# Sixteen experts in fp32 on one Trainium2 core: units of 64 tokens on two strips instead of units of 32 on four

## The chip, the cores and the metric

One core of one Trainium2 chip runs the kernel. The metric is device time in microseconds (us): the kernel before takes 1808.73 us, the median of 3 runs that lie between 1807.75 and 1811.84.

## The reference, cut to what matters

Two decoder layers over 576 tokens (512 of a prompt, 64 of a sample) of width 1024. Each layer is a mixer (convolution and forgetting attention in layer 0, sparse attention in layer 1), and behind it a mixture of experts, which the change concerns. All is float32.

```python
# hier_moe: m = 576 tokens, d = 1024, 16 experts with a hidden width of 512
g_w, g_idx = lax.top_k(softmax(x2 @ w_group + b_group), 1)        # one group of four
top_v, top_i = lax.top_k(e_logits[inside that group], 2)          # two experts inside it
combine = one_hot(expert_id) weighted by softmax(top_v) * g_w
for e in range(16):
    hid = silu(x2 @ w_gate[e]) * (x2 @ w_up[e])
    y = y + combine[:, e:e+1] * (hid @ w_down[e])
```

Each token is in two experts, so there are 1152 pairs of a token and an expert in a layer, spread unevenly.

## The kernel before, in words

The expert stage stands once in each layer. The sixteen experts are taken in 16 steps. Step s has room for `32 * UNITS[s]` tokens, with `UNITS = (3, 3, 5, 2, 4, 2, 4, 2, 3, 3, 2, 3, 3, 2, 3, 3)`, 47 units of 32 in all, and the experts are laid on steps by their size. Tokens beyond that room would go through `spilled`, which has turns of its own.

For each step GpSimd gathers the token rows from DRAM (`xg`, one indirect DMA; a second one for the step of five units), TensorE transposes them in eight 128-column pieces (`turn_x`, L1045), VectorE multiplies them by the norm's gain on the way out of the banks (`inputs`, L1981, into `xgt`). The weights of a step are three blocks of 2 MB (gate, up, down); they are streamed by SyncE into two sets of slots, and the load of a block for step s waits until the last unit of step s-2 has used the same slot (L506). SP issues them in order, so a wait for one block holds all that follow.

TensorE then takes one unit g (32 tokens) after another (`experts`, L1076). A unit is:

- gate: 8 chunks of the width x 4 strips. The stationary operand is 32 tokens x 128 rows, and the moving operand 128 columns of the weights. Strip j of the array (32 of its columns) makes features 128j to 128j+127, so four matmuls with an output of 32 partitions each stand side by side (`group_features`, L1068, the matmul on L1072).
- `turn_hid(g-1)`: one 128x128 transposition of the hidden tile of the unit before (L1084). In the last unit of a step, `turn_x` for the next step stands right behind it (L1115), and so ahead of up.
- up: as gate, into another bank.
- `down(g-1)`: 4 chunks x 4 strips with 256 moving columns (L1096), for the unit before.

In fp32 the profile records each of these matmuls twice, with a weight load (LDWEIGHTS) before each. So a unit has 64 + 64 + 32 = 160 recorded matmuls and as many weight loads.

ScalarE makes silu of gate (L1515), copies down's result to one of four buffers `y2` (L1506) and issues its store to DRAM, `expert_rows`. VectorE copies the transposed hidden tile (`turned`, L1989), multiplies silu by up (L2003), and does the inputs of the next step before that product (L1999). At the stage's start it also builds the token lists of steps 2 to 15: `list_places` for five token tiles behind units 0, 1 and 2; TensorE sums them in `lists` behind `down` (L1123 to L1130) and `list_order` (L1909) gives GpSimd the row numbers for the gather of step 2 and of all later ones. Only steps 0 and 1 start without these lists. After the last unit, `combine` gathers each token's two rows and adds them.

All engines wait on semaphore counts that are written out by hand, by unit number.

Of the kernel before, what the change touches and what calls it, by code (L numbers as in the profile page):

```python
# [26 lines left out]
NT = 5  # L27
# [9 lines left out]
NE = 16  # L37
# [20 lines left out]
GROUPS = sum(UNITS)  # L58
NROWS = 32 * GROUPS
STEP_OF = tuple(s for s in range(NE) for _ in range(UNITS[s]))  # L60
# [34 lines left out]
for _n, _w in (("H", NT * D), ("XT", DC * TOK), ("RING", RING * 4096), ("CR", 8192), ("A3", NT * 512),  # L95
# [9 lines left out]
    (sum(UNITS), "gate_mm up_mm down_mm silu hid ht_mm ht_ev y_ev"),  # L105
# [16 lines left out]
              "y_rows": tuple(16 * len(range(i, sum(UNITS), 4)) for i in range(4))}  # L122
# [13 lines left out]
def trunk(nc, a, o):  # L136
# [161 lines left out]
    y2 = [at("X", 5632 + 256 * i, 256) for i in range(4)]  # L298
    sil2, hid2, ht2 = [[at("X", c + 128 * i, 128) for i in range(2)] for c in (6656, 6912, 7168)]
# [107 lines left out]
    def _(sp):  # L407
# [86 lines left out]
        def experts(l):  # L494
# [33 lines left out]
        for b, name in ((3, "gate_mm0"), (1, "up_mm0"), (2, "down_mm0")):  # L528
            k = first_block(1, "in") + b
            sp.wait_ge(S(name), upto(name, FIRST[14] + UNITS[14]))  # L530
# [54 lines left out]
    def _(pool):  # L585
# [110 lines left out]
        def combine(l):  # L696

            pool.wait_ge(S(f"row_u{l}"), upto(f"row_u{l}", 1))
            for i in range(4):
                pool.wait_ge(S(f"y_rows{l}_{i}"), upto(f"y_rows{l}_{i}", 16 * len(range(i, GROUPS, 4))))  # L700
# [37 lines left out]
    def _(pe):  # L738
# [329 lines left out]
        def group_features(b, w, x):  # L1068

            for c in range(DC):  # L1070
                for j in range(4):
                    last = mm(bank(b, 0, 128, 32 * j, 32 * j + 32), x[:, c, :], w[:, c, 128 * j:128 * j + 128],  # L1072
                              start=(c == 0), stop=(c == DC - 1))
            return last

        def experts(l):  # L1076
# [5 lines left out]
            def turn_hid(g):  # L1082
                pe.wait_ge(S(f"hid{l}"), upto(f"hid{l}", g + 1))
                pe.transpose(bank(1 + g % 2, 128, 256), hid2[g % 2], ident).then_inc(S(f"ht_mm{l}"), 1)  # L1084

            def down(g):
                s = STEP_OF[g]
                if g == FIRST[s]:
# [13 lines left out]
            for g in range(GROUPS):  # L1102
                s = STEP_OF[g]
                u = g - FIRST[s]
                x = xgt[s % 2][:, :, 32 * u:32 * u + 32]
                if u == 0:
# [4 lines left out]
                group_features(0, g3(slot[s % 2][0], DC), x).then_inc(S(f"gate_mm{l}"), 1)  # L1111
# [4 lines left out]
                if u == 0:  # L1116
# [3 lines left out]
                group_features(1 + g % 2, g3(slot[s % 2][1], DC), x).then_inc(S(f"up_mm{l}"), 1)  # L1120
# [217 lines left out]
    def _(act):  # L1338
# [160 lines left out]
        def experts(l):  # L1499

            def store(g):
                i = g % 4
# [3 lines left out]
                af(y2[i], bank(3, 0, 256), ACT.Copy).then_inc(S(f"y_ev{l}"), 1)  # L1506
                act.wait_ge(S(f"y_ev{l}"), upto(f"y_ev{l}", g + 1))
                act.dma_start(y_d[32 * g:32 * g + 32, :].rearrange("t (q c) -> q t c", q=4), y2[i])\
                    .then_inc(S(f"y_rows{l}_{i}"), 16)

            for g in range(GROUPS):
# [3 lines left out]
                af(sil2[g % 2], bank(0, 0, 128), ACT.Silu).then_inc(S(f"silu{l}"), 1)  # L1515
# [4 lines left out]
        def spilled(l):  # L1520
            act.wait_ge(S(f"turns{l}"), upto(f"turns{l}", 1))
            for i in range(4):
# [923 lines left out]
```

## Time and profile before

| what | value |
|---|---|
| median of 3 runs | 1808.73 us |
| the profiled execution's own time | 1802.01 us |
| its span in the profile | 1800.2 us |
| TensorE busy (matmul) | 1475.0 us, 82% |
| TensorE instructions | 20035 matmuls, 20036 weight loads |
| VectorE, ScalarE, GpSimd busy | 652.6, 309.8, 146.8 us |
| TensorE matmuls on L1072 (gate and up) | 12032, 412.9 us |
| TensorE matmuls on L1096 (down) | 3008, 196.8 us |
| mean granted clock | 0.921 of 2.4 GHz |

A matmul's duration is its latency: those of different strips overlap, so busy times of lines are not shares of a whole. "issue" as a releaser of idle time means that no semaphore, engine or DMA in the profile released the instruction. The expert stages lie at about 528 to 884 us (layer 0) and 1405 to 1755 us (layer 1) of the span.

### The profile page before, as it was taken

The numbers are of one execution on the slowest core, as the hardware profiler recorded it, in microseconds if no ns is written. First come the engines' busy times: TensorE is split into PE (matmuls) and PEld (weight loads), VectorE is DVE, ScalarE is ACT, GpSimd is POOL, SyncE is SP. The second block draws the span as 40 slices with busy tenths as digits, with TensorE's granted clock in tenths as the row PEclk, the third lists the DMA queues.
The fourth block names the chain that finished last, engine by engine and source line by source line (L and its number), as shares of the span: only waits on it lengthen the run. The fifth ranks groups of instructions, "written<-read, shape, count | busy, mean of one in ns | idle before, by whom it ended". The sixth has DMA issues, their size and how long they took to land.

```text
span 1800.2 us, 46758 instructions
## 1 busy us (share of the span) xinstructions
PE 1475.0 (82%) x20035; PEld 958.8 (53%) x20036; DVE 652.6 (36%) x1574; ACT 309.8 (17%) x816; POOL 146.8 (8%) x370
## 2 busy tenths in 40 slices
PE   4999968889968988888459998888997798878880
PEld 2444534454467766767344333545545676766670
DVE  2029944331244211111155898665203431111114
ACT  2110024320100000000111211455301000000011
POOL 0039200000000000000110000000000100000002
PEclk9999878889859999999879998898996899999995
DMA  9131128774247788898520031333413568899945
GB/s 358 39 108 48 53 82 227 223 234 197 71 166 287 266 323 325 319 366 334 209 75 23 24 108 60 95 95 95 188 47 146 185 235 323 302 360 343 331 172 173
DMA packets 89531, 342.75 MB, mean 190 GB/s; under 512 B 22751, under 2 KB 39743, under 8 KB 75358
## 3 DMA queue, kind: packets, MB, share of 16 engines
q1 hardware_dynamic: 66254, 289.80, 44.8%
q0 software_dynamic: 10656, 37.56, 6.1%
q10 hardware_dynamic: 12408, 12.32, 2.0%
q8 instruction: 162, 2.65, 0.6%
q14 instruction: 51, 0.42, 0.1%
HBM read 309.53 MB, written 30.47 MB: 189 GB/s over the span
## 4 chain that ended last, share of the span: by engine, by line
PE 61%; DVE 16%; issue 9%; SPq 6%; DMA 4%; ACT 3%; POOL 1%; POOLq 0%; DVEq 0%; ACTq 0%
PE banks L1072 21%; PE banks L1096 9%; PE banks L1011 8%; DVE arena L2077 6%; PE banks L784 5%; PE banks L813 4%; SPq L438 3%; DVE arena L1626 3%; SPq L464 2%; PE banks L766 2%; PE banks L930 1%; PE banks L1051 1%; DMA arena<-expert_rows,arena 1%; PE banks L1084 1%; SPq L469 1%
## 5 line engine op out<-in xcount | busy, mean ns | idle before, releaser
L1072 PE MATMUL banks<-arena 128*32 128x128 f32 x12032 | 412.9, 278 | 76.4 <-issue 74.1
L1072 PEld LDWEIGHTS banks<-arena 128*32 128x32 f32 x12032 | 353.4, 111 | 115.8 <-issue 94.8
L1096 PE MATMUL banks<-arena 128*32 128x256 f32 x3008 | 196.8, 384 | 24.3 <-issue 23.5
L784 PE MATMUL banks<-arena 128*128 128x512 f32 (+1 forms) x400 | 174.0, 594 | 0.0
L1992 DVE COPY arena<-banks 128x128 f32<-128x128 f32 x94 | 27.4, 291 | 374.0 <-PE banks L1084 362.5
L1626 DVE TENSOR_TENSOR arena<-arena,banks 128x128 f32<-128x128 f32 (+4 forms) x118 | 44.1, 374 | 324.2 <-PE banks L1072 177.4
L1096 PEld LDWEIGHTS banks<-arena 128*32 128x32 f32 x3008 | 119.1, 111 | 65.8 <-issue 30.2
L813 PE MATMUL banks<-arena 128*128 128x512 f32 (+1 forms) x320 | 145.9, 602 | 0.0
L1011 PE MATMUL banks<-arena 128*128 128x512 f32 (+1 forms) x320 | 138.8, 594 | 1.4 <-issue 0.8
L1626 DVE TENSOR_TENSOR arena<-arena 128x256 f32<-128x256 f32 (+17 forms) x248 | 99.0, 432 | 87.7 <-ACT arena L1379 66.1
L784 PEld LDWEIGHTS banks<-arena 128*128 128x128 f32 (+1 forms) x400 | 70.7, 179 | 100.3 <-issue 100.2
L1626 DVE TENSOR_TENSOR arena<-banks,arena 128x512 f32<-128x512 f32 (+5 forms) x159 | 70.4, 473 | 138.9 <-ACT arena L1431 85.8
L1506 ACT ACTIVATE arena<-banks 128x256 f32<-128x256 f32 x94 | 36.0, 383 | 433.3 <-PE banks L1096 433.3
L2077 DVE SCALAR_TENSOR_TENSOR arena<-arena 128x512 f32<-128x512 f32 x120 | 105.2, 937 | 1.1
L1011 PEld LDWEIGHTS banks<-arena 128*128 128x128 f32 (+1 forms) x320 | 56.7, 179 | 82.1 <-issue 81.4
L813 PEld LDWEIGHTS banks<-arena 128*128 128x128 f32 (+1 forms) x320 | 55.6, 181 | 73.8 <-issue 72.2
L751 PE MATMUL banks<-arena 128*128 128x128 f32 (+1 forms) x160 | 29.6, 357 | 70.1 <-DVE arena L1656 70.1
L674 POOL DMA_INDIRECT arena<-hn_scratch,arena x32 | 29.5, 922 | 604.5 <-PE banks L1051 474.4
L1515 ACT ACTIVATE arena<-banks 128x128 f32<-128x128 f32 x94 | 26.1, 277 | 232.5 <-PE banks L1072 220.9
L751 PEld LDWEIGHTS banks<-arena 128*128 128x128 f32 (+1 forms) x160 | 25.9, 199 | 73.6 <-DVE arena L1656 51.5
L1414 ACT ACTIVATE arena<-arena 128x128 f32<-128x128 f32 (+3 forms) x96 | 53.0, 556 | 26.8 <-DVE arena L1675 26.8
L839 PE MATMUL banks<-arena 64*128 64x128 f32 (+3 forms) x192 | 41.1, 508 | 18.2 <-DVE arena L1675 16.8
(268 smaller groups left out, 1440.4 us busy)
## 6 DMA issues: line engine op xcount, KB each, us to landing
arena<-in_wstream SPq DMA_DIRECT2D x109, 2048.0 KB, 11.2
arena<-in_fox_kt SPq DMA_DIRECT2D x64, 256.0 KB, 3.0
arena<-in_fox_v SPq DMA_DIRECT2D x64, 256.0 KB, 3.0
arena<-in_dsa_page SPq DMA_DIRECT2D x64, 256.0 KB, 3.0
expert_rows<-arena ACTq DMA_DIRECT2D x94, 128.0 KB
expert_rows<-arena POOLq DMA_DIRECT2D x1, 6656.0 KB, 33.3
hn_scratch<-arena POOLq DMA_DIRECT2D x8, 512.0 KB, 3.7
arena<-in_x_prompt SPq DMA_DIRECT2D x1, 2048.0 KB, 10.0
```

Source lines behind the costliest of these rows:

```text
L438: return sp.value_load(pages[0:1, NPG * s + j:NPG * s + j + 1], min_val=0, max_val=a["n_pool"] - 1)
L464: sp.dma_start(g3(k_even[s % 2], NPG)[:, j, :], page_rows(a["fox_kt"], page_id(s, j)))\
L751: last = pe.transpose(bank(b, 128 * (c % 4), 128 * (c % 4) + rows(t)), hn[t % 2][0:rows(t), 128 * c:128 * c + 128], ident[0:rows(t), 0:row ...
L784: last = mm(bank(job % 4, 0, 512, 0, rows(t)), xt[:, c, c0:c1], w[:, c, :], start=(c == 0), stop=(c == DC - 1))
L813: last = mm(bank(job % 2, 0, 512, 0, rows(t)), xt[:, c, c0:c1], w[:, c, :], start=(c == 0), stop=(c == DC - 1))
L839: last = mm(bank(a, 0, n), q(2 * p + a)[:, 128 * t:128 * t + 128], k(2 * p + a)[:, 0:n], start=True, stop=(l == 1))
L1011: last = mm(bank(job % 4, 0, 512, 0, rows(t)), xt[:, c, c0:c1], w[:, c, :], start=(c == 0), stop=(c == DC - 1))
L1072: last = mm(bank(b, 0, 128, 32 * j, 32 * j + 32), x[:, c, :], w[:, c, 128 * j:128 * j + 128], start=(c == 0), stop=(c == DC - 1))
L1096: last = mm(bank(3, 0, 256, 32 * q, 32 * q + 32), ht2[g % 2][:, 32 * c:32 * c + 32], w[:, c, 256 * q:256 * q + 256], start=(c == 0), stop= ...
L1414: af(x, x, ACT.Exp, bias=mx[:, c:c + 1], scale=-1.0, accum_out=esum[:, c:c + 1])\
L1626: return v.tensor_tensor(out, x, y, op)
L2077: last = v.scalar_tensor_tensor(out=op, in0=ip, scalar=w, in1=op, op0=ALU.mult, op1=ALU.add)
```

## The change

A step's tokens are now taken in parts: as many of 64 tokens as fit, and a last one of 32 where `UNITS[s]` is odd. That makes 28 parts a layer (19 of 64 and 9 of 32) in place of 47 units. A part of 64 uses a stationary operand of 64 tokens on two strips of 64 columns each, with 256 moving columns in gate and up and 512 in down; a part of 32 is as before. `y2` becomes two buffers of twice the width. The transpositions of the next step's tokens move behind up (ahead of `down(g-1)`), and VectorE's inputs behind the product. The building of lists is packed into fewer, larger parts.

```diff
+PARTS = tuple((s, 64 * i, min(64, 32 * UNITS[s] - 64 * i)) for s in range(NE) for i in range((UNITS[s] + 1) // 2))
+GROUPS = len(PARTS)
+ENDS = tuple(sum((u + 1) // 2 for u in UNITS[:s + 1]) for s in range(NE))
...
-    y2 = [at("X", 5632 + 256 * i, 256) for i in range(4)]
+    y2 = [at("X", 5632 + 512 * i, 512) for i in range(2)]
...
-                    sp.wait_ge(S(name), upto(name, FIRST[s - 2] + UNITS[s - 2]))
+                    sp.wait_ge(S(name), upto(name, ENDS[s - 2]))
...
-        def group_features(b, w, x):
+        def part_features(b, w, x, n):
             for c in range(DC):
-                for j in range(4):
-                    last = mm(bank(b, 0, 128, 32 * j, 32 * j + 32), x[:, c, :], w[:, c, 128 * j:128 * j + 128],
+                for j in range(128 // n):
+                    last = mm(bank(b, 0, 4 * n, n * j, n * j + n), x[:, c, :], w[:, c, 4 * n * j:4 * n * j + 4 * n],
                               start=(c == 0), stop=(c == DC - 1))
...
             def turn_hid(g):
                 pe.wait_ge(S(f"hid{l}"), upto(f"hid{l}", g + 1))
-                pe.transpose(bank(1 + g % 2, 128, 256), hid2[g % 2], ident).then_inc(S(f"ht_mm{l}"), 1)
+                for i in range(PARTS[g][2] // 32):
+                    last = pe.transpose(bank(1 + g % 2, 256 + 128 * i, 384 + 128 * i),
+                                        hid2[g % 2][:, 128 * i:128 * i + 128], ident)
+                last.then_inc(S(f"ht_mm{l}"), 1)
...
                 for c in range(4):
-                    for q in range(4):
-                        last = mm(bank(3, 0, 256, 32 * q, 32 * q + 32), ht2[g % 2][:, 32 * c:32 * c + 32],
-                                  w[:, c, 256 * q:256 * q + 256], start=(c == 0), stop=(c == 3))
+                    j, i = divmod(c, n // 32)
+                    for q in range(128 // n):
+                        last = mm(bank(3, 0, 8 * n, n * q, n * q + n), ht2[g % 2][:, 128 * i + n * j:128 * i + n * j + n],
+                                  w[:, c, 8 * n * q:8 * n * q + 8 * n], start=(c == 0), stop=(c == 3))
...
-                if u == UNITS[s] - 1 and s + 1 < NE:
-                    turn_x(l, s + 1)
-                if u == 0:
+                if off == 0:
                     landed(s, 1)
                 if g > 1:
                     pe.wait_ge(S(f"ht_ev{l}"), upto(f"ht_ev{l}", g - 1))
-                group_features(1 + g % 2, g3(slot[s % 2][1], DC), x).then_inc(S(f"up_mm{l}"), 1)
+                part_features(1 + g % 2, g3(slot[s % 2][1], DC), x, n).then_inc(S(f"up_mm{l}"), 1)
+                if g == 2:
+                    for t in range(1, NT):
+                        lists(l, t)
+                if g == ENDS[s] - 1 and s + 1 < NE:
+                    turn_x(l, s + 1)
                 if g > 0:
                     down(g - 1)
                 if g == 1:
                     lists(l, 0)
-                if g == 2:
-                    lists(l, 1)
-                    lists(l, 2)
-                if g == 3:
-                    lists(l, 3)
-                    lists(l, 4)
...
+                i, r0 = g % 2, 32 * FIRST[s] + off
-                if g >= 4:
-                    act.wait_ge(S(f"y_rows{l}_{i}"), upto(f"y_rows{l}_{i}", 16 * (g // 4)))
+                if g >= 2:
+                    act.wait_ge(S(f"y_rows{l}_{i}"), upto(f"y_rows{l}_{i}", 16 * (g // 2)))
...
                 if g > 0:
                     turned(g - 1)
-                if g == FIRST[s] + UNITS[s] - 1 and s + 1 < NE:
-                    inputs(s + 1)
                 dve.wait_ge(S(f"up_mm{l}"), upto(f"up_mm{l}", g + 1))
                 dve.wait_ge(S(f"silu{l}"), upto(f"silu{l}", g + 1))
+                tt(hid2[g % 2][:, 0:4 * n], sil2[g % 2][:, 0:4 * n], bank(1 + g % 2, 0, 4 * n), ALU.mult)\
+                    .then_inc(S(f"hid{l}"), 1)
+                if g == ENDS[s] - 1 and s + 1 < NE:
+                    inputs(s + 1)
...
                 if g == 1:
-                    list_places(l, 1)
-                    list_places(l, 2)
+                    for t in range(1, NT):
+                        list_places(l, t)
                 if g == 2:
-                    list_places(l, 3)
-                    list_places(l, 4)
-                if g == 3:
                     list_order(l)
```

## Rows read from the trace of the kernel before

**Rows 1.** Stretches: length, busy of each engine (records), granted clock, DMA share, GB/s.

```profile
528.00:884.00 356.00, 304.90 (x7770) 250.49 (x7770) 63.35 (x177) 31.05 (x94) 13.72 (x15) 0.97 0.80 300
1405.00:1755.00 350.00, 298.06 (x7770) 245.72 (x7770) 63.38 (x177) 31.04 (x94) 13.71 (x15) 0.99 0.77 287
```

**Rows 2.** Groups by line, 528 to 884 us: count, busy, mean ns, idle before.

```profile
L1072 PE MATMUL banks<-arena 128*32 128x128 f32 x6016 | 208.9, 280 | 39.2 <-issue 38.0 <-DVE arena L1626 1.1
L1096 PE MATMUL banks<-arena 128*32 128x256 f32 x1504 | 99.7, 386 | 10.8 <-issue 10.4 <-DVE arena L1992 0.4
```

**Rows 3.** The same groups, 1405 to 1755 us.

```profile
L1072 PE MATMUL banks<-arena 128*32 128x128 f32 x6016 | 204.0, 276 | 37.2 <-issue 36.1 <-DVE arena L1626 1.1
L1096 PE MATMUL banks<-arena 128*32 128x256 f32 x1504 | 97.1, 381 | 13.5 <-issue 13.1 <-DVE arena L1992 0.4
```

**Rows 4.** DMA queues, 528 to 885 us: packets, MB, share of 16 engines.

```profile
q1 hardware_dynamic: 6480, 94.37, 68.6%
...
q0 software_dynamic: 1552, 5.37, 4.7%
q8 instruction: 61, 1.00, 1.2%
```

**Rows 5.** Timeline, 610 to 650 us: start, length, instructions, idle before and releaser.

```profile
630.99 0.35 PEld L1096 LDWEIGHTS banks<-arena 128*32 128x32 f32 x9 [2.09 <-issue]
...
637.19 0.25 PEld L1072 LDWEIGHTS banks<-arena 128*32 128x32 f32 x9 [1.96 <-issue]
...
639.16 2.12 PE L1072 MATMUL banks<-arena 128*32 128x128 f32 x64
...
641.22 0.33 PE L1084 MATMUL banks<-arena 128*128 128x128 f32 x1
...
645.24 2.12 PE L1072 MATMUL banks<-arena 128*32 128x128 f32 x64
```

**Rows 6.** Chain that ended last, 1395 to 1445 us: start, length, what.

```profile
1398.13 4.20 DMA arena<-hn_scratch,arena
...
1412.03 1.88 PE banks L1072 x64
1413.91 1.73 PE banks L1096 x32
...
1417.96 0.26 PE banks L1084
1418.22 0.66 PE banks L1051 x8
...
1432.82 9.08 DMA arena<-hn_scratch,arena
```

**Rows 7.** Groups by line and shape, 408 to 413 us: the attention's two-strip matmuls.

```profile
L870 PE MATMUL banks<-arena 128*64 128x128 f32 x16 | 1.1, 279 | 0.0
L870 PEld LDWEIGHTS banks<-arena 128*64 128x64 f32 x16 | 0.9, 136 | 0.2 <-issue 0.2
```

**Rows 8.** Timeline, 1130 to 1150 us, TensorE: the sample's values on two strips.

```profile
1133.97 2.33 PE L930 MATMUL banks<-arena 128*64 128x128 f32 x36
```

**Rows 9.** Timeline, 1395 to 1470 us: units and lists at the stage's start.

```profile
1411.96 1.95 PE L1072 MATMUL banks<-arena 128*32 128x128 f32 x64
...
1422.97 0.50 PE L1038 MATMUL banks<-arena 128*128 128x1 f16 x14
...
1431.54 0.36 DVE L1626 TENSOR_TENSOR arena<-arena,banks 128x196 f32<-128x196 f32 x1 [2.51 <-PE banks L1040]
```

**Rows 10.** DMA queues, 706 to 724 us, a stretch of full load.

```profile
q1 hardware_dynamic: 441, 6.36, 89.4%
```

**Rows 11.** By tile, the whole span, the experts' rows: issue to landing.

```profile
DMA to landing us min/median/max: 4.0/5.4/33.3
```

**Rows 12.** Groups by line and shape, 528 to 884 us: VectorE's lists and inputs.

```profile
L1626 DVE TENSOR_TENSOR arena<-arena 128x1792 f16<-128x1792 f16 x5 | 9.9, 2018 | 0.0
L1626 DVE TENSOR_TENSOR arena<-banks,arena 128x512 f32<-128x512 f32 x6 | 3.9, 686 | 2.3 <-PE banks L1051 1.2 <-PE banks L1056 1.2
```

More of the change, by code:

```diff
@@ L57 @@
 FIRST = tuple(sum(UNITS[:s]) for s in range(NE))
-GROUPS = sum(UNITS)
-NROWS = 32 * GROUPS
-STEP_OF = tuple(s for s in range(NE) for _ in range(UNITS[s]))
+NROWS = 32 * sum(UNITS)
+PARTS = tuple((s, 64 * i, min(64, 32 * UNITS[s] - 64 * i)) for s in range(NE) for i in range((UNITS[s] + 1) // 2))
+GROUPS = len(PARTS)
+ENDS = tuple(sum((u + 1) // 2 for u in UNITS[:s + 1]) for s in range(NE))
 def most_spills():
@@ L104 @@
 SHARED = (
-    (sum(UNITS), "gate_mm up_mm down_mm silu hid ht_mm ht_ev y_ev"),
+    (GROUPS, "gate_mm up_mm down_mm silu hid ht_mm ht_ev y_ev"),
     (NE, "xgt xg_used"),
@@ L121 @@
 PER_PARITY = {"hn_out": (48, 32), "yb": (48, 48, 32, 32),
-              "y_rows": tuple(16 * len(range(i, sum(UNITS), 4)) for i in range(4))}
+              "y_rows": tuple(16 * len(range(i, GROUPS, 2)) for i in range(2))}
 def first_block(layer, part):
@@ L297, in trunk @@
     xgt = [g3(at("X", 2048 + 1280 * i, 1280), DC) for i in range(2)]
-    y2 = [at("X", 5632 + 256 * i, 256) for i in range(4)]
-    sil2, hid2, ht2 = [[at("X", c + 128 * i, 128) for i in range(2)] for c in (6656, 6912, 7168)]
+    y2 = [at("X", 5632 + 512 * i, 512) for i in range(2)]
+    sil2, hid2, ht2 = [[at("X", c + 256 * i, 256) for i in range(2)] for c in (6656, 7168, 7680)]
     yout = at("X", 4608, 1024)
@@ L529, in _ @@
             k = first_block(1, "in") + b
-            sp.wait_ge(S(name), upto(name, FIRST[14] + UNITS[14]))
+            sp.wait_ge(S(name), upto(name, ENDS[14]))
             sp.dma_start(ring[k % RING], a["wstream"][k]).then_inc(S(f"ring{k % RING}"), 16)
@@ L698, in combine @@
             pool.wait_ge(S(f"row_u{l}"), upto(f"row_u{l}", 1))
-            for i in range(4):
-                pool.wait_ge(S(f"y_rows{l}_{i}"), upto(f"y_rows{l}_{i}", 16 * len(range(i, GROUPS, 4))))
+            for i in range(2):
+                pool.wait_ge(S(f"y_rows{l}_{i}"), upto(f"y_rows{l}_{i}", 16 * len(range(i, GROUPS, 2))))
             for t in range(NT):
@@ L1101, in experts @@
             turn_x(l, 0)
[L1102 to L1105, printed above, removed]
-                if u == 0:
+            for g, (s, off, n) in enumerate(PARTS):
+                x = xgt[s % 2][:, :, off:off + n]
+                if off == 0:
                     pe.wait_ge(S(f"xgt{l}"), upto(f"xgt{l}", s + 1))
@@ L1110, in experts @@
                     pe.wait_ge(S(f"silu{l}"), upto(f"silu{l}", g))
-                group_features(0, g3(slot[s % 2][0], DC), x).then_inc(S(f"gate_mm{l}"), 1)
+                part_features(0, g3(slot[s % 2][0], DC), x, n).then_inc(S(f"gate_mm{l}"), 1)
                 if g > 0:
                     turn_hid(g - 1)
-                if u == UNITS[s] - 1 and s + 1 < NE:
-                    turn_x(l, s + 1)
-                if u == 0:
+                if off == 0:
                     landed(s, 1)
@@ L1514, in experts @@
                     act.wait_ge(S(f"hid{l}"), upto(f"hid{l}", g - 1))
-                af(sil2[g % 2], bank(0, 0, 128), ACT.Silu).then_inc(S(f"silu{l}"), 1)
+                af(sil2[g % 2][:, 0:4 * n], bank(0, 0, 4 * n), ACT.Silu).then_inc(S(f"silu{l}"), 1)
                 if g > 0:
@@ L1521, in spilled @@
             act.wait_ge(S(f"turns{l}"), upto(f"turns{l}", 1))
-            for i in range(4):
-                act.wait_ge(S(f"y_rows{l}_{i}"), upto(f"y_rows{l}_{i}", 16 * len(range(i, GROUPS, 4))))
+            for i in range(2):
+                act.wait_ge(S(f"y_rows{l}_{i}"), upto(f"y_rows{l}_{i}", 16 * len(range(i, GROUPS, 2))))
             def turn(n):
@@ L2019, in experts @@
                     row_keys(l)
+                if g == 5:
+                    spill_lists(l)
                 if g == 6:
-                    spill_lists(l)
-                if g == 7:
                     spill_blocks(l)
-                if g == 8:
                     row_numbers(l)
```

18 lines of the change are left out of this document (8 added, 10 removed).

## The prediction

> **What bounds the kernel now.** I read the stretches of the two expert stages first, then their groups by line, the DMA queues, the timeline of a steady piece, and the chain that ended last. The stages take 356 and 350 of 1800 us, TensorE is busy in 86% of each at nearly full clock (0.97 and 0.99), and the DMA engines in 80 and 77% [rows 1]. No engine hands TensorE anything late: of the 50.0 us that it idles before gate, up and down in layer 0, 48.4 have the releaser "issue" [rows 2], in layer 1 49.2 of 50.7 [rows 3]. These gaps lie inside a group of matmuls, between two that wait for no semaphore, are about 2 us long and come again 6.2 us later [rows 5]. What they are, the queues show: the queue for instructions moved 61 packets and 1.00 MB in layer 0 [rows 4], so 16 KB each, and TensorE has 7770 matmuls and as many loads there [rows 1], 15540 / 61 = 255 instructions for each packet. I read them as TensorE having used up its 255 instructions before the next packet came. Without gaps a unit takes 645.24 - 639.16 = 6.08 us [rows 5] and has about 322 instructions, so a packet lasts 6.08 x 256 / 322 = 4.8 us; with the mean gap (48.4 / 61 = 0.8 us) a refill under the weights' load takes some 5.6 to 6.2 us.
>
> So a stage is 47 units of 6.08 us (286), 49 us of instruction gaps, the rest transpositions of tokens, lists and the start.
>
> **Matmuls of a part of 64.** A matmul on four strips: 64 of them end in 1.95 us [rows 9], less the last one's own 0.27 (the rows' means are 276 to 280 ns) that is (1.95 - 0.27) / 63 = 26.7 ns each, so each strip streams 128 columns in 107 ns. Down takes 1.73 us for 32 of 256 columns [rows 6], 54 ns each, so 216 ns on a strip: the same rate. Two strips of 64 are in the attention: 16 with 128 columns in 1.1 us [rows 7], (1.1 - 0.27) / 15 = 55 ns, 110 on a strip, and 36 in 2.33 [rows 8], (2.33 - 0.27) / 35 = 59 ns. Nearly the same rate per column again, with 3 to 11 ns lost per matmul on a strip, and with twice the columns there is less of that. A part of 64 has 32 + 32 + 16 records of 107, 107 and 214 ns: 3 x 3.42 = 10.3 us. The two units that it replaces stream 2 x (1.71 + 1.71 + 1.73) = 10.3 us. The streaming itself gains nothing.
>
> What is saved is once per unit: 6.08 - 5.15 = 0.93 us of draining before and behind the transposition, and the transposition (0.26 [rows 6]). A part of 64 pays it once, with a second transposition and a longer last matmul, about 1.15 us: 11.4 against 12.16 us. I take 0.75 us saved for each of the 19 parts, 14 us a layer (nothing, if the two-strip rate of 59 ns holds for 256 columns too, where 64 records would lose some 6 ns each on gate and up, 0.4 us a part and 7 us a layer, and the drain is longer; up to 18 if not).
>
> The row on the two-strip form also decides a question that one rule raises. Its 16 weight loads take 0.9 us while the 16 matmuls take 1.1 [rows 7], so they run beside each other, though all use all 128 rows. The Trainium skill (TensorE: Matmul & The Clock Gate, "Part 3: Packing small matmuls") says that a weight load overlaps with matmuls in flight only when its row group differs. By that rule the loads here would stand in line with the matmuls, and the change would lose; the trace disagrees with it. I keep it as a rival, priced from the rows.
>
> **Instruction gaps.** A part of 64 has 80 matmuls and 80 loads where two units had 640 instructions. A layer goes from 47 x 160 = 7520 matmuls to 19 x 80 + 9 x 160 = 2960; the other 250 stay. That is 6420 instructions, 25 packets instead of 61. In a part of 64 a packet lasts 11.4 x 256 / 164 = 17.8 us, three times the refill: no gap. In a part of 32 it lasts 4.8 us as before, but that part has 1.3 packets' worth, and its neighbour is a part of 64, so a gap needs two packet ends inside it. Nine such parts with, say, four gaps of 1 us: 4 us stay. Gone: about 45 us a layer (between 49, and 35 if a refill becomes slower because the weights fill the queues more densely).
>
> **Transpositions of the tokens behind up.** Before, they shared one drain with the hidden tile's transposition: eight of 96 tokens added 0.66 us [rows 6]. Now they stand between up and down, each with a drain of its own. From gate's start to the transposition is 641.22 - 639.16 = 2.06 us where 1.71 are streamed [rows 5], so 0.35 us, and as much again at most for the way back. 15 x 0.4 = 6 us a layer added (3 to 11). VectorE's inputs (two of 0.69 us for 128 tokens [rows 12]) then have down to hide under, 3.4 us behind a part of 64, 1.73 behind one of 32, where they just fit, with the product ahead of them.
>
> **The start.** The gather of step 2 waits for the lists. Their matmuls are 0.5 us for each token tile; from the last of them to the gather's issue is 1432.82 - 1431.54 = 1.3 us, and the gather landed after 9.08 us under load [rows 6, 9]. Before, a unit and a gate lay between. Now lists 1 to 4 stand behind up of part 2, and until the transpositions that need the gather there are down (1.73), gate (2.06), transposition (0.26) and up (1.8): about 6.2 us with drains, against 1.3 + 9.1 = 10.4 us, so up to 4.2 us of new wait. The idle queues of the stage before took 4.2 us for a gather [rows 6], which would hide it. Load 2 of step 2 waits for the same down, so the queues are half empty when the gather starts. I take 3 us a layer (0 to 4.2, and to 7 if the clock falls after it). The four `list_places` of 2.02 us each [rows 12] lie under gate and up of part 2 (7 us) with 2 to 3 us to spare.
>
> **Weights.** In the full stretch a load's queue moved 6.36 MB in 18 us [rows 10], 5.9 us for a block of 2.1 MB when the gathers and stores run beside it; 94.37 MB in 68.6% of 356 us [rows 4] is 5.4 us. A step needs three: 16 to 18 us. A step of two units is now one part, about 12 us with its transpositions; one of three 18.5, one of four 24. A short step leaves a debt of 4 to 6 us, and two sets of slots let the neighbours pay it. Also down's slot is freed one gate and one up of 64 later (7 us instead of 4), and the next step's loads queue behind it on SP. I followed the 42 loads in order, each starting when its slot is free and the load before it is through: at 5.4 us a load TensorE never waits, at 5.9 it waits some 10 us a layer, all at the gate and up of steps 11 and 14, each of which follows a short step. I take 4 us a layer; bounds 0 and 20 (all five short steps at 4 us each).
>
> **At nothing.** ScalarE's silu and copy, VectorE's product and transposed copy become twice as wide and half as many; each has a whole gate or up of 3.4 us above it. Two `y2` buffers: a store waits for that of two parts before, 17 us earlier, and stores land after 5.4 us in the median [rows 11]; if the cover went, down would wait. The waits of `combine` are as before.
>
> **Sum.** Per layer -14 - 45 + 6 + 3 + 4 = -46; two layers -92 us. The profiled execution took 1802.0 us itself and becomes 1710. The median of the runs stands 6.7 us above it (1808.7), so a run would be 1710 to 1717: I say 1713 us.
>
> **Rivals.**
> - The weights become the bound: the stage moves 107 MB in 356 us at 80% busy [rows 1, 4]; at 304 us the same work is 94% busy. For it: short steps have a debt each. Against: two slots, and the loads wait for the slots now, not the other way. At 15 to 20 us a layer instead of 4: +28, 1741 us.
> - The gaps are not the instructions, or they stay in number: a cause that follows time (the DMA load) leaves them. For it: they come only while weights are streaming. Against: 255 instructions to a packet, and their distance. Then only -14 + 6 + 3 is left, -5 a layer: 1799 us.
> - Slower: on two strips the weight load isn't hidden. 0.9 us / 16 = 53 ns for each of 1520 records is 81 us a layer, 162 in all; with the -92 that gives 1879 us. The sign turns when 30 of the 53 ns are exposed (92 us / 3040). Against it stand both attention rows; for it only that their moving operand is half as wide.
>
> **Chances.** Forecast 0.70, weights 0.15, gaps stay 0.10, loads exposed 0.05. The forecast's own range is 1695 to 1730; the weights' case and the known terms at their bad ends push the upper end to 1745, the lower end is 1692 (all gaps gone, 18 saved by handovers, no new waits). Outside are the last two cases. A measurement here tells 0.2% (3.6 us) from no change. Faster 0.93 (all but the last case and a fifth of the third), same 0.02, slower 0.05.
>
> **What would show it.** TensorE's matmul records fall from 20035 to about 10900; the instruction queue moves about 25 packets in a stage; idle before gate, up and down with the releaser "issue" falls below 10 us a layer. A part of 64 takes 11 to 12 us from gate to gate. The wait of the transpositions for the gather of step 2 stands in the chain. The weights' share of the DMA rises above 75% in a stage. The prediction is wrong if the two-strip matmuls come at more than 115 ns each, if "issue" stays above 25 us a layer, or if TensorE waits for the weights by more than 15 us a layer.

## The result, and the profile after

The changed kernel takes 1859.33 us (median of 4 runs, 1854.39 to 1878.58) against 1808.24 (4 runs, 1797.48 to 1811.84) of the kernel before: a ratio of 1.031, interval 1.023 to 1.040. It is slower by 51 us where 95 us less were forecast. The profiled execution took 1859.95 us, its span is 1858.1 us.

The page of the kernel after: the queues of part 3 (packets, MB, share of 16 engines), the chain's shares, and the groups of part 5.

```profile
PE 1457.5 (78%) x10915; PEld 801.4 (43%) x10916; DVE 639.4 (34%) x1498; ACT 297.1 (16%) x740; POOL 145.1 (8%) x370
...
q10 hardware_dynamic: 7316, 12.32, 1.8%
q8 instruction: 90, 1.47, 0.3%
...
PE 39%; DMA 30%; DVE 17%; SPq 6%; issue 4%; ACT 3%; POOL 1%; POOLq 0%; DVEq 0%; ACTq 0%
...
L1073 PE MATMUL banks<-arena 128*32 128x128 f32 (+1 forms) x4736 | 356.6, 335 | 4.9 <-DVE arena L1627 2.7
L1101 PE MATMUL banks<-arena 128*64 128x512 f32 (+1 forms) x1184 | 196.6, 550 | 162.6 <-ACT arena L1507 162.6
...
L1507 ACT ACTIVATE arena<-banks 128x512 f32<-128x512 f32 (+1 forms) x56 | 29.6, 529 | 599.7 <-DMA expert_rows<-arena 429.0
```

Two things are to be seen. What the prediction wanted gone is gone: 10915 matmuls, and gate and up (L1073) idle 4.9 us in both layers, where they idled 39.2 + 37.2 = 76.4 us [rows 2, 3]. And something new stands on down (L1101): 162.6 us behind ScalarE's copy of the part before (L1507), which in turn waits 429 us for a store, `expert_rows`. By the prediction's own -92 us and this wait the execution would have taken 1802 - 92 + 163 = 1873 us; it took 1860. So the rest of the sum comes out within 13 us in total, and one line under "At nothing" cost 163 us.

The stages in the view by stretches (columns as in [rows 1]): 400 and 367 us long, and both the clock and the DMA share are lower than in [rows 1].

```profile
530.00:930.00 400.00, 293.71 (x3210) 171.48 (x3210) 57.03 (x139) 24.61 (x56) 13.72 (x15) 0.86 0.69 266
1448.00:1815.00 367.00, 294.44 (x3210) 172.05 (x3210) 56.76 (x138) 24.61 (x56) 13.72 (x15) 0.90 0.71 272
```

The timeline of a bad stretch, 598 to 720 us (start, length, engine, line, idle before and its releaser):

```profile
616.65 3.67 PE L1073 MATMUL banks<-arena 128*64 128x256 f32 x32
620.15 3.60 PE L1101 MATMUL banks<-arena 128*64 128x512 f32 x16
...
652.69 0.60 ACT L1507 ACTIVATE arena<-banks 128x512 f32<-128x512 f32 x1 [35.60 <-DMA expert_rows<-arena]
...
653.43 6.28 PE L1101 MATMUL banks<-arena 128*64 128x512 f32 x16 [21.60 <-ACT arena L1507]
```

ScalarE waits 35.6 us before it may overwrite the `y2` buffer. The bank of `down` is not free until it has copied, so TensorE stands for 21.6 us, and then runs its 16 matmuls in 6.28 us instead of 3.60. The chain that ended last (start, length, what) says the same: stores of 40 to 50 us, one behind the other, with `down` and other matmuls between them.

```profile
603.22 49.38 DMA expert_rows<-arena
...
653.43 6.28 PE banks L1101 x16
...
672.42 40.35 DMA expert_rows<-arena
...
719.48 40.06 DMA expert_rows<-arena
```

### The profile page after: what moved, and what is told of

It is laid out like the page before. It is cut to its first block, busy times and chain, and to the rows that moved or that the text cites. A ratio compares the mean times of both kernels' runs of the same rounds, so it can differ in the third digit from the quotient of the medians.

```text
span 1858.1 us, 28138 instructions
## 1 busy us (share of the span) xinstructions
PE 1457.5 (78%) x10915; PEld 801.4 (43%) x10916; DVE 639.4 (34%) x1498; ACT 297.1 (16%) x740; POOL 145.1 (8%) x370
## 3 DMA queue, kind: packets, MB, share of 16 engines
q10 hardware_dynamic: 7316, 12.32, 1.8%
## 4 chain that ended last, share of the span: by engine, by line
PE 39%; DMA 30%; DVE 17%; SPq 6%; issue 4%; ACT 3%; POOL 1%; POOLq 0%; DVEq 0%; ACTq 0%
DMA expert_rows<-arena 26%; PE banks L1012 7%; PE banks L1073 7%; DVE arena L2075 6%; PE banks L1101 5%; PE banks L785 5%; DVE arena L1627 3%; SPq L439 3%; PE banks L814 3%; DMA arena<-hn_scratch,arena 2%; DVE arena L1759 1%; PE banks L767 1%; SPq L465 1%; DMA arena<-expert_rows,arena 1%; SPq L470 1%
## 5 line engine op out<-in xcount | busy, mean ns | idle before, releaser
L1073 PE MATMUL banks<-arena 128*32 128x128 f32 (+1 forms) x4736 | 356.6, 335 | 4.9 <-DVE arena L1627 2.7
L1101 PE MATMUL banks<-arena 128*64 128x512 f32 (+1 forms) x1184 | 196.6, 550 | 162.6 <-ACT arena L1507 162.6
L1073 PEld LDWEIGHTS banks<-arena 128*32 128x32 f32 (+1 forms) x4736 | 239.1, 126 | 121.2 <-issue 39.3
L1627 DVE TENSOR_TENSOR arena<-arena,banks 128x256 f32<-128x256 f32 (+5 forms) x80 | 38.2, 479 | 488.8 <-ACT arena L1516 233.3
L1101 PEld LDWEIGHTS banks<-arena 128*64 128x64 f32 (+1 forms) x1184 | 67.1, 137 | 259.5 <-issue 248.6
L1507 ACT ACTIVATE arena<-banks 128x512 f32<-128x512 f32 (+1 forms) x56 | 29.6, 529 | 599.7 <-DMA expert_rows<-arena 429.0
L1994 DVE COPY arena<-banks 128x256 f32<-128x256 f32 (+1 forms) x56 | 21.4, 382 | 274.3 <-PE banks L1086 267.9
L1348 ACT ACTIVATE arena<-arena 128x1024 f32<-128x1024 f32 (+1 forms) x20 | 21.1, 1056 | 160.2 <-DVE arena L1627 131.7
## 6 DMA issues: line engine op xcount, KB each, us to landing
expert_rows<-arena POOLq DMA_DIRECT2D x1, 6656.0 KB, 33.3
```

What stands on the lines that cost most here:

```text
L1073: last = mm(bank(b, 0, 4 * n, n * j, n * j + n), x[:, c, :], w[:, c, 4 * n * j:4 * n * j + 4 * n], start=(c == 0), stop=(c == DC - 1))
L1101: last = mm(bank(3, 0, 8 * n, n * q, n * q + n), ht2[g % 2][:, 128 * i + n * j:128 * i + n * j + n], w[:, c, 8 * n * q:8 * n * q + 8 * n], ...
L1507: af(y2[i][:, 0:8 * n], bank(3, 0, 8 * n), ACT.Copy).then_inc(S(f"y_ev{l}"), 1)
L1627: return v.tensor_tensor(out, x, y, op)
```

## Why a store takes 40 us

Each store goes through ScalarE's queue, q10. Its packet count tells how many DMA engines work on one store, if each that takes part adds one small packet at the end. Data are 128 packets a store in both kernels: 32 tokens x 4 strips of 1 KB before, 64 x 2 of 2 KB after (a part of 32 as before). From the page of the kernel before:

```profile
q10 hardware_dynamic: 12408, 12.32, 2.0%
```

Before, 94 stores made 12408 packets, which is 94 x (128 + 4). After, 56 stores made 7316: 56 x 128 = 7168 and 148 more, which is 38 x 2 + 18 x 4 for the 38 parts of 64 and the 18 of 32. The packets' sizes bear the reading out (from the trace's packets, no view shows them): the queue has exactly 94 x 4 = 376 packets of 4 bytes before and 148 after, and all others are of 1 or 2 KB.

So 4 engines of 16 carried a store of 32 tokens, and 2 carry one of 64. The number is that of the strips: the store is written `y_d[...].rearrange("t (q c) -> q t c")`, with the strip as its outermost dimension. The Trainium skill (DMA: Bandwidth & Descriptors, "Why a DMA increments its semaphore by 16 and not by 1") has this as a rule: the number of engines is the largest k up to 16 that divides the outermost dimension longer than 1 on both sides. The packet counts agree (k = 4 and 2).

The second half is the load of the weights. The queues of the kernel after in 680 to 696 us, with a store under way on two engines, and of the kernel before in 672 to 684 us:

```profile
q1 hardware_dynamic: 452, 6.64, 97.9%
q10 hardware_dynamic: 50, 0.10, 1.6%
```

```profile
q1 hardware_dynamic: 325, 4.70, 92.8%
q10 hardware_dynamic: 82, 0.08, 2.0%
```

After, an engine moved 452 / 16 = 28 weight packets and 50 / 2 = 25 store packets in the same time; before, 325 / 16 = 20 and 82 / 4 = 20. An engine takes about one small piece for each 16 KB piece of weights, one per 0.6 us. A store of 64 tokens has 64 pieces on each of its engines, 64 x 0.6 = 38 us; one of 32 tokens has 32, some 20 us. The Trainium skill (DMA: Bandwidth & Descriptors, "Queues, rings and completion order") says that an engine goes round its queues packet by packet. The counts agree with the turns. They do not show the size that the page calls typical for a packet, 9 to 17 descriptors: here the store's pieces come one at a time, some 0.7 us apart (from the trace's packets at 620 to 632 us).

The times at which each buffer's semaphore rose also give for each store the time from the copy's end to its landing (no view shows it). Before, the median is 12.4 us and the longest 28.7, under a cover of four buffers, 4 units of 356 / 47 = 7.5 us, so 30 us. After, the median is 21.8 and the longest 49.4, under a cover of two parts. The longest is the store of 603.22 us in the chain above: the one before it held both engines until 615.1 us, and its own 64 pieces on each then took until 652.1, so 37 us. With no weights beside it a store of 32 tokens takes 3.3 us on 4 engines, and one of 64 tokens 7.8 us on 2. Bytes and data packets of all stores together were the same; the engines and the number of buffers were halved.

## Experiments

The theories: (S) a store is slow because its strips put it on 2 engines that the weights share, and down waits for it; (B) the two buffers alone are at fault; (T) the transpositions behind up, with the wait for ScalarE, delay the chain; (W) the weights bound the stage. The expectations on record have letters of their own: theory A is the wait of ScalarE's copy for the stores, theory D is (S), and "the weights bind" is (W).

**Four wide buffers.**

```diff
-    y2 = [at("X", 5632 + 512 * i, 512) for i in range(2)]
+    y2 = [at("X", 5632, 512), at("X", 6144, 512), at("QT", 4096, 512), at("XT", 4096, 512)]
```

> The changed kernel with four row buffers of 512 columns instead of two; two of them lie at the end of regions that the expert stage leaves free (QT and XT from column 4096). Nothing else is changed. Theory A (the loss is the wait of ScalarE's copy for the store of two parts before, so buffers are what is short): the wait of the copy for the stores falls from 429 us in both layers to under 20, TensorE's idle time before down with releaser ACT from 163 us to under 10, and the time is 1700 to 1730 us, where the prediction had it. Rival B (the stores are a bandwidth of their own, too slow for the stage, and more buffers only move the wait to the end): the wait at the end of the stage grows, and the time stays above 1790. Rival C (the weights bind once the stores do not): 1740 to 1760, with waits for the weights before gate and up of steps 11 and 14.

Measured: 1835.1 us, ratio 1.019 (1.015 to 1.024). Buffers alone give back 24 us, about a sixth of the 146 us between the kernel after and the forecast. The copy's wait for the stores is gone from the view of waits, as theory A expected, but the time is not: rival B of the expectation, that buffers only move the wait, is what the run shows. The timeline of ScalarE, and the issues of its stores (min/median/longest of one, ns):

```profile
642.38 29.09 ACTq L1509 DMA_DIRECT2D expert_rows<-arena  x1
671.58 0.38 ACT L1516 ACTIVATE arena<-banks 128x256 f32<-128x256 f32 x1 [29.23 <-issue]
```

```profile
L1509 ACTq DMA_DIRECT2D expert_rows<-arena x56: 521/1096/29095, 544.1 to 1780.8; - x56
```

The kernel before, in the same view:

```profile
L1508 ACTq DMA_DIRECT2D expert_rows<-arena x94: 547/547/1175, 540.7 to 1754.5; - x94
```

ScalarE now hangs in the issue itself, up to 29.1 us: with several stores of 64 pieces an engine ahead, the next could, as I read it, not be put into the queue. The landings became longer (median 34.0, longest 60.4 us), and TensorE waited at gate and up instead, 122 us in both layers, behind the silu. More buffers move this wait, they do not remove it.

**The kernel before with two buffers.**

```diff
-    y2 = [at("X", 5632 + 256 * i, 256) for i in range(4)]
+    y2 = [at("X", 5632 + 256 * i, 256) for i in range(2)]
```

> The kernel before (units of 32 on four strips) with two row buffers of 256 columns instead of four, nothing else changed. Theory A: a store is waited for by the copy of two units later, 15 us, while in the trace of before many stores took 20 to 28 us from issue to their last packet; TensorE waits at down in the loaded stretches, 40 to 90 us in both layers, time 1850 to 1900 us. Rival (the long landings come only with stores of 64 tokens on two strips, 256 KB each): landings stay as before, median 12 us, the wait is under 15 us in all and the time is within 1% of before.

Measured: 1843.17 us (one run), 41 more than the 1802.06 beside it. The view of waits, both layers (us in total, times, longest):

```profile
ACT arena L1506 <- DMA expert_rows<-arena: 228.1, 20, 18.8
...
PE banks L1096 <- ACT arena L1506: 57.1, 12, 8.5
```

TensorE waits 57 us at down for the copy, inside the 40 to 90 expected; the time is 7 us under its range. The old cover of 30 us was needed: its stores took up to 28.7.

**A quarter of each weight load, in the kernel after.** Steps 2 to 15 load only the first quarter of the columns.

```diff
-weights(l, s, i, a["wstream"][bass.ds(k + (b + i), 1)].rearrange("a p w -> (a p) w"))
+sp.dma_start(slot[s % 2][i][:, 0:1024], a["wstream"][bass.ds(k + (b + i), 1), :, 0:1024].rearrange("a p w -> (a p) w"))
```

> The changed kernel, two row buffers, but the weight loads of steps 2 to 15 fetch only the first 1024 of 4096 columns of each block (a quarter of the bytes; the rest of a slot keeps what it held), so the stores share the DMA engines with a quarter of the traffic. Theory A with its cause (a store is slow because the weight loads fill the engines): stores land in about 8 us, the time of one alone, the copy no longer waits, and the kernel takes 1690 to 1720 us. Rival (a store of this shape is slow by itself or by its number in the queue): landings stay above 15 us in the median and the time above 1800.

Measured: 1673.01 us (one run). By line and shape:

```profile
L1102 PE MATMUL banks<-arena 128*32 128x256 f32 x576 | 37.3, 403 | 6.3 <-ACT arena L1508 6.3
```

Down's wait falls from 162.6 to 6.3 us and the landings to a median of 8.5 us, with the stores of 64 tokens still on two engines. So it takes both: few engines, and weights on them.

**The old place of the transpositions, with four buffers.** `turn_x(l, s + 1)` right behind `turn_hid(g - 1)`, `inputs(s + 1)` right behind `turned(g - 1)`, the rest as in the first experiment.

> Four wide row buffers, and the transpositions of the next step's tokens back ahead of up, with VectorE's inputs back ahead of the product, as in the kernel before. Measured against the kernel with four buffers alone. Prediction's term: the place behind up costs 0.4 us at each of 15 steps, 6 us a layer, so this kernel is 8 to 14 us faster than the other (0.5 to 0.8%), less what the gather of step 2 now makes it wait (it is needed 4 us earlier: up to 8 us in two layers back). Rival: the place is worth nothing, both within 3 us.

Measured: 1843.21 us, ratio 1.024 (1.021 to 1.027), 8 us slower than with the new place, with intervals that overlap. Nothing comes back, so (T) falls.

**Stores cut by strip, in the kernel after, two buffers kept.** Two DMAs for a part of 64, four for one of 32; each has the token as its outermost dimension.

```diff
-                act.dma_start(y_d[r0:r0 + n, :].rearrange("t (q c) -> q t c", q=128 // n), y2[i][:, 0:8 * n])\
-                    .then_inc(S(f"y_rows{l}_{i}"), 16)
+                for q in range(128 // n):
+                    act.dma_start(y_d[r0:r0 + n, 8 * n * q:8 * n * q + 8 * n], y2[i][n * q:n * q + n, 0:8 * n])\
+                        .then_inc(S(f"y_rows{l}_{i}"), 16)
```

> The changed kernel with its two row buffers, and each store split by strip: a part of 64 goes out in two DMAs (rows of 64 tokens by 512 columns, partitions 0 to 63 and 64 to 127), one of 32 in four. Same bytes, same 2 KB or 1 KB pieces, the same 128 pieces. Theory D (one store as written, with the strip as the outermost dimension of its DRAM side, runs on as many DMA engines as that dimension has, 2 or 4, and there each piece waits behind a 16 KB piece of the weights, 0.6 us: 64 x 0.6 = 39 us for a part of 64, 32 x 0.6 = 20 us for 32; split, the outermost dimension is 64 or 32 tokens and all 16 engines take part, 4 to 8 pieces each): stores land in 4 to 8 us also under load, the copy never waits for them, the kernel takes 1700 to 1730 us. Rival (the stores' queue gets little service beside the weights, on whatever engines): landings stay over 15 us in the median under load and the time over 1800. The Trainium skill (DMA: Bandwidth & Descriptors, on how many engines a DMA takes) gives the rule of theory D: the largest number up to 16 that divides the slowest dimension of both sides.

Measured: 1704.18 us (1698.2 to 1714.37), ratio 0.947 (0.944 to 0.951). This one edit takes 155 us off the changed kernel. From its page:

```profile
q10 hardware_dynamic: 9536, 12.33, 2.2%
q8 instruction: 90, 1.47, 0.4%
...
PE 54%; DVE 19%; DMA 15%; SPq 4%; issue 4%; ACT 3%; POOL 1%; ACTq 0%; POOLq 0%; DVEq 0%
```

9536 = 7168 + 148 x 16: the same 7168 data packets, and 148 DMAs with 16 engines each. From the copy's end to the last landing of a part the median is 11.9 us and the longest 15.0 (21.8 and 49.4 before this edit). That is slower than the 4 to 8 us expected, but under the cover, two parts of 299 / 28 = 10.7 us. ScalarE's copy waits for no store, and no down of 64 waits (groups by shape):

```profile
L1079 PE MATMUL banks<-arena 128*64 128x256 f32 x2432 | 289.3, 393 | 23.9 <-issue 10.9 <-DMA arena<-in_wstream 10.8 <-DVE arena L1634 2.2
...
L1107 PE MATMUL banks<-arena 128*64 128x512 f32 x608 | 138.2, 596 | 0.0
...
L1079 PE MATMUL banks<-arena 128*32 128x128 f32 x2304 | 73.9, 278 | 2.4 <-issue 2.4
...
L1107 PE MATMUL banks<-arena 128*32 128x256 f32 x576 | 36.3, 394 | 1.1 <-ACT arena L1513 1.1
L1058 PE MATMUL banks<-arena 96*128 96x96 f32 x128 | 15.3, 268 | 11.0 <-DMA arena<-hn_scratch,arena 11.0
```

**The same cut in the kernel before.** Four DMAs per unit, `y_d[32*g:32*g+32, 256*q:256*q+256]` from `y2[i][32*q:32*q+32, :]`.

> The kernel before with each of its stores (32 tokens, four strips, four row buffers) split into four DMAs by strip. Theory D: landings fall from a median of 12 us to about 4 and from at most 28 to below 10; no wait was there to remove, so the time changes little: 1795 to 1812 us, with three more DMA issues of 0.55 us on ScalarE in each unit, which have 4 us of cover. What it could gain: the weights' loads are spread evenly again (up to 10 us less instruction gaps). Rival: landings stay as before.

Measured: 1812.05 us, ratio 1.005 (1.002 to 1.009). Its queue shows 18048 packets, 12032 + 376 x 16, as it should with 16 engines each; the median landing of a unit falls from 12.4 to 9.9 us and the longest from 28.7 to 17.4, not to the 4 and under 10 us expected. It gains nothing (if anything it is 0.5% slower), since four buffers hid the stores before. So the 155 us are no gain of the cut as such; they are the debt that the change had made.

**The cut with the old place of the transpositions, and the cut with four buffers.** The edits are those of the fourth and the first experiment on top of the cut.

> As e5 (changed kernel, stores by strip), with the transpositions of the next step's tokens and VectorE's inputs back where the kernel before had them, ahead of up and of the product. Read against e5. The prediction's term says that the place behind up costs 6 us a layer and that the earlier place makes the gather of step 2 wait up to 4 us longer each: 4 to 12 us faster than e5. Rival (shown by the two kernels with four buffers, 1835 and 1843 us): the earlier place is slower, by 5 to 10 us.

> Stores by strip and four wide row buffers. Theory D: no wait for the stores is left with two, so this is e5 within 3 us. Rival: two buffers still cost a wait in the loaded stretches, and this kernel is 10 us or more faster than e5.

Measured: 1702.14 us, ratio 0.946 (0.943 to 0.949), and 1704.92 us, ratio 0.945 (0.942 to 0.949). Neither can be told from the cut alone. Theory (B) falls with the second: once stores use all engines, two buffers are as good as four. The sign of (T) is not to be told from the first: 2 us faster here, 8 us slower without the cut.

**Each store as two DMAs by columns, the strip still outermost.** It tells whether the gain of the cut was that there are more DMAs.

```diff
-                act.dma_start(y_d[r0:r0 + n, :].rearrange("t (q c) -> q t c", q=128 // n), y2[i][:, 0:8 * n])\
-                    .then_inc(S(f"y_rows{l}_{i}"), 16)
+                for c0 in (0, 4 * n):
+                    act.dma_start(y_d[r0:r0 + n, :].rearrange("t (q c) -> q t c", q=128 // n)[:, :, c0:c0 + 4 * n],
+                                  y2[i][:, c0:c0 + 4 * n]).then_inc(S(f"y_rows{l}_{i}"), 16)
```

> The changed kernel, two row buffers, with each store split in two DMAs by columns instead of by strip: the strip is still the outermost dimension of each (2 for a part of 64, 4 for one of 32), the pieces are half as long and twice as many, the bytes are the same. It is the counterpart of the split by strip. Theory D (few engines, and there one piece after each piece of the weights): 128 pieces on each of two engines, so landings in a loaded stretch go from 40 towards 77 us, and the time from 1859 to 1950 or more. The queue's packets are 56 x 256 and, for the counts of engines 2 and 4, 38 x 2 x 2... that is 2 x 148 more for the semaphores, 14336 + 296 = 14632. Rival E (what helped the split by strip was two smaller DMAs in place of one, so that they come between the weights): the time falls here too, below 1800.

Measured: 1873.96 us (one run), 14 more than the kernel after's 1859.33. Its page, its waits in both layers, and its issues:

```profile
q10 hardware_dynamic: 14632, 12.32, 2.0%
```

```profile
ACT arena L1507 <- DMA expert_rows<-arena: 88.5, 24, 14.2
```

```profile
L1510 ACTq DMA_DIRECT2D expert_rows<-arena x112: 522/585/23452, 551.9 to 1823.8; - x112
```

14632 = 56 x 256 + 2 x 148: twice the data packets, and still 2 or 4 engines a DMA. More DMAs are not what helped: rival E expected less than 1800. ScalarE stands mostly in the issue here, up to 23.5 us, and less in the wait for a buffer. My own size missed, though: twice the pieces did not double the price. The expectation wanted landings towards 77 us and 1950 us or more; the longest landing is 41 us. In a stretch of 16 us in which the weights moved at 75.7% instead of 98%, I read the cause in part: when TensorE stands, no slot comes free, the loads stop, and the stores drain alone. The wait brakes what causes it.

**A quarter of each weight load, in the kernel before.** The edit of the third experiment.

> The kernel before, with the weight loads of steps 2 to 15 reduced to the first 1024 of 4096 columns of each block (the rest of a slot keeps what it held). Theory of the instruction gaps (TensorE uses up 16 KB of instructions in 4.8 us, and a refill takes 5.6 to 6.2 us when the weights fill the DMA queues): a refill is quicker, the idle time with releaser issue before gate, up and down falls from 99 us in both layers to under 20, the time from 1803 to 1705 to 1730 us. Rival (the gaps are not refills, or a refill is slow by itself): they stay, and the time is within 15 us of before.

Measured: 1677.28 us, ratio 0.928 (0.922 to 0.934). By line and shape, and from its page:

```profile
L1073 PE MATMUL banks<-arena 128*32 128x128 f32 x12032 | 388.4, 276 | 9.1 <-issue 6.8 <-DVE arena L1627 2.2
...
L1097 PE MATMUL banks<-arena 128*32 128x256 f32 x3008 | 187.8, 382 | 1.4 <-DVE arena L1993 0.8 <-issue 0.5
```

```profile
q8 instruction: 161, 2.64, 0.6%
```

The kernel before has 162 such packets, but 98 us of gaps instead of 7.3. The other factor was varied above: with half the instructions beside the full stream, 13.3 us stay. Both are what the prediction's reading asks for, that a gap is a refill of instructions which the weights slow down; the refill itself stands in no view. The time is 28 us under the lower end of what I expected, and the durations show where that was. The same matmuls of gate, up and down are busy 388.4 + 187.8 us here and 412.9 + 196.8 in the kernel before, 33.5 us more, at the same granted clock of 0.97 in layer 0. So a part of the delay stood in the matmuls' durations and not in their idle time. From the first gate to the last down the stages take 295.8 and 290.2 us, for 355.2 and 349.0 in the kernel before: 118 us, where the idle time fell by 90.

## Why the prediction was wrong

**The step that failed** is, in the part "At nothing": "Two `y2` buffers: a store waits for that of two parts before, 17 us earlier, and stores land after 5.4 us in the median [rows 11]; if the cover went, down would wait." The sentence names the right consequence and rests on the wrong number. The row [rows 11] is for all DMAs of the tile `expert_rows`: its landings are those of GpSimd's one clearing store (33.3 us) and of `combine`'s gathers. The 94 stores of ScalarE have none there: their issue line in the kernel before, shown with the first experiment, ends in "- x94". I took a median of 5.4 us that belonged to other transfers; in truth it was 12.4 us, with a longest of 28.7, right under the 30 us of cover that four buffers gave. The true median would still have fitted under the 17 us; it is the longest stores that do not, and those on half the engines. Half the cover alone costs the kernel before 41 us; with half the engines it cost 163 us of down's time. What would have told was readable: 12408 packets for 94 stores is 132 each, hence 4 engines, and the new expression makes that 2.

None of the rivals named this cause. The one on the other side had exposed weight loads; they are not exposed. It came near in time (1879) by accident.

**The other steps**, read in the changed kernel with the stores cut, which is the forecast's case (1704 measured, 1713 forecast):

- Streaming and handovers, -14 a layer: too large. From gate to gate a part of 64 takes 620.96 - 610.05 = 10.91 us.

```profile
610.05 3.67 PE L1079 MATMUL banks<-arena 128*64 128x256 f32 x32
...
617.53 3.60 PE L1107 MATMUL banks<-arena 128*64 128x512 f32 x16
...
620.96 3.62 PE L1079 MATMUL banks<-arena 128*64 128x256 f32 x32
...
628.49 0.71 PE L1058 MATMUL banks<-arena 64*128 64x64 f32 x8
...
632.62 3.62 PE L1079 MATMUL banks<-arena 128*64 128x256 f32 x32
```

  Against two units of 6.08 that looks like 1.25 saved. But the unit of [rows 5] was not free of delay: at the end of layer 1 the kernel before has units of 1745.69 - 1740.07 = 5.62 us. With a quarter of the weights most of its units without a turn of tokens take 5.62 or 5.80.

```profile
1740.07 1.93 PE L1072 MATMUL banks<-arena 128*32 128x128 f32 x64
...
1745.69 1.93 PE L1072 MATMUL banks<-arena 128*32 128x128 f32 x64
```

  So a part of 64 saves 2 x 5.62 - 10.91 = 0.33 us where I had 0.75: 19 x 0.33 = -6 a layer.
- Instruction gaps, -45 a layer: right in kind, too small. Of 97.6 us of idle time [rows 2, 3], 13.3 stay in both layers (10.9 and 2.4 in the rows above), so -42 a layer; the instruction queue has 90 packets against 162 in the whole span. The delay that stood in the durations comes on top; the experiment with the kernel before puts both together at 118 / 2 = 59 a layer, nearly all of it gone.
- Transpositions behind up, +6: too large. A part with the turn of 64 tokens takes 632.62 - 620.96 = 11.66 us, 0.75 more, of which the matmuls themselves are 0.71; the old place is 2 us faster with the cut and 8 slower without it, so no cost of the place is shown.
- The gather of step 2, +3: too large. The 11.0 us in the row above (L1058, 96 tokens) are the wait for the gather of step 0 at the start of each stage, and the kernel before has it too, 5.26 and 5.33 us. Step 2, the one of five units, waits 1.08 us in layer 0 and 0.80 in layer 1:

```profile
525.18 1.52 PE L1058 MATMUL banks<-arena 96*128 96x96 f32 x8 [5.33 <-DMA arena<-hn_scratch,arena]
...
567.11 0.68 PE L1063 MATMUL banks<-arena 32*128 32x32 f32 x8 [1.08 <-DMA arena<-hn_scratch,arena]
```

- The weights, +4: TensorE waits 10.8 us for them in both layers, so 5.4 a layer: about right.

From the first gate to the last down, the stages of four runs give the balance of both layers. The kernel before takes 355.2 + 349.0 us and with a quarter of the weights 295.8 + 290.2, 118 less. The change with a quarter of the weights takes 290.1 + 282.8, another 13 less. With the full weights and the stores cut it takes 299.5 + 298.9, 25 more, and 10.8 us of waits for weights and 13.3 of gaps stand against that. That is -106 in all; the profiled execution fell by 1802.0 - 1698.9 = 103 us. So what the change is worth here is almost all in the instruction gaps. That the total is 9 us from the forecast is in part luck, since errors cancelled: the gain of the handovers was too large by 8 us a layer, the costs of transpositions and gather too large by 6 and 2, and the gain of the gaps too small by the part in the durations. The stages in the view by stretches:

```profile
528.00:825.00 297.00, 283.81 (x3178) 167.61 (x3176) 57.15 (x138) 23.97 (x55) 13.73 (x15) 0.97 0.91 355
1353.00:1650.00 297.00, 283.34 (x3202) 167.30 (x3198) 57.32 (x138) 24.40 (x56) 13.71 (x15) 0.98 0.87 336
```

These windows miss some 2 us of each stage. The DMA engines are busy at 91 and 87% in them, for 80 and 77% in [rows 1]. The weights are the next bound: in the chain that ended last they stand with single steps of 22 us,

```profile
628.75 21.91 DMA arena<-in_wstream
```

and the kernel that loads a quarter of them is at 1673 us even with stores on two engines. (W) was no cause of the loss, but little is left above it. The rival of the exposed loads is ruled out by these rows: 32 matmuls of 128x64 take 3.6 us, where streaming alone was priced at 3.42.

**What stays open**: how much ScalarE's queue holds before an issue stands; why landings stay at a median of 11.9 us with 16 engines; and whether the place of the transpositions matters at all.

## What to carry to other kernels

When a change reshapes a tile, look at the outermost dimension of every DMA that reads or writes it: here it fell from 4 to 2 and with it the engines that carried the store, at the same bytes and the same packets. Divide a queue's packets by its DMAs, and see what is left beyond the data; and before a buffer is taken away, find the time of just those transfers under the load that they run beside, from their own packets if the view has no landing for them. A cost put at nothing because it is hidden needs its cover measured against the longest case, not the median of a row that may belong to others. And a row that is taken as free of delay has to be the shortest of its kind: the unit of 6.08 us was not.

## What the runs showed of the hardware

- A store of 256 KB alone takes 7.8 us on 2 engines, one of 128 KB 3.3 us on 4; beside the full weight stream up to 49 us (12 of them behind the store ahead) and 29 us. An engine moved one store piece per 16 KB weight piece, about one per 0.6 to 0.7 us, whether the piece was 1 or 2 KB.
- ScalarE's DMA issue, 0.55 us in the median of the kernel before, stood for up to 29.1 us with several slow stores ahead, and everything of ScalarE behind it stood too.
- Behind the wait of 21.6 us the granted clock was 0.58 of 2.4 GHz, mostly the lower level of 1.2, and 16 matmuls of down took 6.28 us; at a clock of 1.00 they took 3.60. The DMA share shows too that the loads stop (stretches of the kernel after, columns as above: the wait, the down behind it, and a down at full clock).

```profile
631.80:653.40 21.60, 0.03 (x1) 0.00 (x1) 0.00 (x0) 0.60 (x1) 0.90 (x1) 0.57 0.72 285
653.40:659.80 6.40, 6.37 (x20) 2.29 (x22) 1.09 (x3) 0.44 (x2) 0.00 (x0) 0.58 0.12 37
620.15:623.70 3.55, 3.55 (x20) 1.26 (x18) 0.42 (x1) 0.00 (x0) 0.00 (x0) 1.00 0.99 412
```

- TensorE's gaps of instruction supply came to about 98 us beside the full weight stream and to 7.3 us beside a quarter of it, at 162 and 161 packets; the same matmuls' durations fell by another 33.5 us.
